# First stage of a transformer block: two weight tiles in halves, low parts of x ahead of the sums of squares, norm's total and spread in the second raw pair

## The reference, cut to what matters

```
def rms_norm(x, g):
    return x * rsqrt(mean(x * x, axis=-1) + EPS) * g
def swiglu(x, w_gate, w_up, w_down):
    return (silu(x @ w_gate) * (x @ w_up)) @ w_down
x = x + 0.5 * swiglu(rms_norm(x, g_ffn1), w_ffn1_gate, w_ffn1_up, w_ffn1_down)
```

## Time and profile before

| what | value |
|---|---|
| median of three runs | 2106.23 us |
| the profiled execution's own time | 2106.04 us |
| its span in the trace | 2103.9 us |
| PE busy | 2088.7 us, 99% of the span |
| DVE busy | 1249.3 us, 59% |
| ACT busy | 793.8 us, 38% |
| POOL busy | 299.6 us, 14% |
| first product of the raw pairs starts | 10.27 us |
| first product of tiles 4 and 5 starts | 35.00 us |

### The profile page before, as it was taken

The page is one execution under the profiler, slowest core; times in us unless marked ns, Lnnn a source line. Parts: engine busy times, 40 slices in busy tenths (PEclk is TensorE's granted clock), DMA queues, the critical chain, the costliest instruction groups (busy, mean ns, idle before and its releaser), DMA issues.

```text
span 2103.9 us, 28233 instructions
## 1 busy us (share of the span) xinstructions
PE 2088.7 (99%) x9928; PEld 1714.0 (81%) x9928; DVE 1249.3 (59%) x1844; ACT 793.8 (38%) x1156; POOL 299.6 (14%) x357
## 2 busy tenths in 40 slices
PE   9999999999999999999999999999999999999999
PEld 8888888887888888877777888888888888888887
DVE  7666544787676654466996676654465466333332
ACT  6222333567432223344365432223343234222222
POOL 0122400650212230024300212210000000000000
PEclk9999999999999999999999999999999999999999
DMA  5565333320345642323300346542323222222232
GB/s 194 180 197 195 93 110 111 118 94 2 110 166 187 198 136 83 96 95 116 102 30 1 110 154 197 190 142 80 97 101 110 91 89 100 100 94 95 76 96 87
DMA packets 79572, 243.32 MB, mean 116 GB/s; under 512 B 12784, under 2 KB 13424, under 8 KB 79376
## 3 DMA queue, kind: packets, MB, share of 16 engines
q1 hardware_dynamic: 61376, 189.61, 27.6%
q0 software_dynamic: 18128, 52.84, 8.1%
HBM read 235.84 MB, written 2.29 MB: 113 GB/s over the span
## 4 chain that ended last, share of the span: by engine, by line
PE 92%; DVE 5%; ACT 1%; POOL 1%; issue 1%; DMA 0%; SPq 0%; ACTq 0%; DVEq 0%; POOLq 0%
PE ps L717 28%; PE ps L719 28%; PE ps L718 28%; PE ps L1027 2%; PE ps L1009 1%; PE ps L988 1%; DVE ps L2012 1%; DVE tmp L1656 1%; DVE small L1910 1%; PE ps L1149 0%; POOL w_lo L626 0%; DVE ropA L1883 0%; PE ps L991 0%; PE ps L933 0%; DVE qA L1885 0%
## 5 line engine op out<-in xcount | busy, mean ns | idle before, releaser
L717 PE MATMUL ps<-h_hi,w_hi 128*128 128x512 f32 x1888 | 740.0, 392 | 1.7 <-DVE h_lo L1955 0.9
L719 PE MATMUL ps<-h_hi,w_lo 128*128 128x512 f32 x1888 | 735.0, 389 | 0.0
L718 PE MATMUL ps<-h_lo,w_hi 128*128 128x512 f32 x1888 | 734.7, 389 | 0.0
L1613 DVE TENSOR_TENSOR w_lo<-w_raw,w_hi 128x1024 fp32r<-128x1024 f32 x336 | 411.4, 1226 | 384.1 <-ACT w_hi L1232 370.1
L1232 ACT ACTIVATE w_hi<-w_raw 128x1024 fp32r<-128x1024 f32 x383 | 402.4, 1052 | 242.5 <-PE ps L719 240.8
L717 PEld LDWEIGHTS ps<-h_hi,w_hi 128*128 128x128 f32 x1888 | 353.7, 187 | 82.4 <-issue 7.7
L719 PEld LDWEIGHTS ps<-h_hi,w_lo 128*128 128x128 f32 x1888 | 353.7, 187 | 75.0
L718 PEld LDWEIGHTS ps<-h_lo,w_hi 128*128 128x128 f32 x1888 | 353.8, 187 | 73.1 <-issue 0.2
L717 PE MATMUL ps<-hid_hi,w_hi 128*128 128x512 f32 x704 | 273.9, 389 | 0.0
L718 PE MATMUL ps<-hid_lo,w_hi 128*128 128x512 f32 x704 | 273.9, 389 | 0.0
L719 PE MATMUL ps<-hid_hi,w_lo 128*128 128x512 f32 x704 | 273.9, 389 | 0.0
(11 more groups left out here) (314 smaller groups left out, 1771.1 us busy)
## 6 DMA issues: line engine op xcount, KB each, us to landing
ada_raw<-in_ada_w POOLq DMA_DIRECT2D x96, 512.0 KB, 4.7
w_raw<-in_gate SPq DMA_DIRECT2D x88, 512.0 KB, 3.5
w_raw<-in_up SPq DMA_DIRECT2D x88, 512.0 KB, 3.2
w_raw<-in_down SPq DMA_DIRECT2D x64, 384.0 KB, 3.1
w_raw<-in_down SPq DMA_DIRECT2D x64, 320.0 KB, 2.9
w_raw<-in_w_mix_c SPq DMA_DIRECT2D x24, 512.0 KB, 3.2
w_raw<-in_w_mix_b SPq DMA_DIRECT2D x17, 512.0 KB, 3.3
w_raw<-in_w_mix SPq DMA_DIRECT2D x16, 512.0 KB, 3.3
```

Of the source, the lines that this page charges most:

```text
L717: pe.matmul(dest, s_hi, m_hi, start=first and n == 0, stop=False)
L718: pe.matmul(dest, s_hi, m_lo, start=False, stop=False)
L719: mm = pe.matmul(dest, s_lo, m_hi, start=False, stop=last and n == len(pairs) - 1)
L1613: dve.tensor_tensor(chunk(w_lo, slot, WT), chunk(w_raw, slot, WT), f32(chunk(w_hi, slot, WT)), ALU.subtract).then_inc(w_lo_done, 1)
```

## The change

The first two weight tiles are loaded, copied and subtracted in halves (chunks 0 to 3, chunks 4 to 7), with semaphores of their own for the first halves, and SP's order becomes: cols, first half of gate 0, x0, first half of up 0, x1, second half of gate 0, x2, second half of up 0, x3, x4, tile 2, x5, x6, x7, tile 3. PE waits for the first halves at chunk 0 and for the second halves at chunk 4. On ACT and DVE the squares and their sums no longer alternate with the high and low parts of x: squares 0 to 3 and sums 0 and 1 stand between the later chunks, and the rest comes after tile 3. The split of tile 3 moves out of `norm` to just before them. PE computes the total after chunk 2 of the second pair (before: chunk 6 of the first) and the spread after chunk 4 of the second pair (before: chunk 0). `idle(30)` becomes `idle(20)`.

```diff
@@ -198,6 +198,9 @@
         x_in = [sem(f"x_in{k}") for k in range(KC)]
         stage_in = sem("stage_in")
         w_in = [sem(f"w_in{s}") for s in range(RING)]
+        w_half_in = [sem(f"w_half_in{s}") for s in range(2)]
+        w_half_hi = sem("w_half_hi")
+        w_half_lo = sem("w_half_lo")
         w_hi_done = sem("w_hi_done")
         w_lo_done = sem("w_lo_done")
         job_done = sem("job_done")
@@ -244,8 +247,8 @@
 
         RAW = {n: first_job[stage] for n, stage in enumerate(("ffn0", "mixA", "ffn1", "mixB", "ffn2", "mixC", "ffn3"))}
         RAW_PAIRS = {n: 2 if n == 0 else 1 for n in RAW}
-        TOTAL_AT = {n: (0, 1) if n else (0, KC - 2) for n in RAW}
-        SPREAD_AT = {n: (0, 2) if n else (1, 0) for n in RAW}
+        TOTAL_AT = {n: (0, 1) if n else (1, 2) for n in RAW}
+        SPREAD_AT = {n: (0, 2) if n else (1, 4) for n in RAW}
         SHIFTED = range(3, 7)
 
         def ada_from(n):
@@ -531,9 +534,16 @@
                         load(J + s, i, 4, tile_of(WEIGHTS[stage], i * 4 + s))
 
             sp.dma_start(cols[:, :], A["cols"]).then_inc(consts_in, 16)
+            def opening_half(s, half, signal):
+                at = half * WT // 2
+                sp.dma_start(w_raw[:, s * WT + at:s * WT + at + WT // 2], A[("gate0", "up0")[s]][0, :, at:at + WT // 2])\
+                    .then_inc(signal, 16)
+
             for k in range(KC):
                 if k < 2:
-                    up_tile(0, 0, k)
+                    opening_half(k, 0, w_half_in[k])
+                elif k < 4:
+                    opening_half(k - 2, 1, w_in[k - 2])
                 sp.dma_start(chunk(x, k), A["x"][k]).then_inc(x_in[k], 16)
                 if k == 4:
                     up_tile(0, 0, 2)
@@ -761,11 +771,17 @@
                     mm.then_inc(p_misc.at(f"shift{n}"), 1)
                 for pair in range(pairs):
                     last = pair == pairs - 1
-                    take(js + 2 * pair + 1)
+                    halved = (n, pair) == (0, 0)
+                    if not halved:
+                        take(js + 2 * pair + 1)
                     for k in range(KC):
                         pe.wait_ge(raw_lo_done, n * KC + k + 1)
+                        if halved and k == KC // 2:
+                            take(js + 1)
                         for s in range(2 * pair, 2 * pair + 2):
                             width = 8 if n == 3 and s == 1 else P
+                            if halved and k == 0:
+                                pe.wait_ge(w_half_lo, s + 1)
                             mm = product(None, bank(s)[0:width, :], [(weights(js + s, k, width),
                                                                        (chunk(hi, k), chunk(lo, k)))], k == 0, k == KC - 1)
                             if k == KC - 1:
@@ -1041,7 +1057,7 @@
                 mm.then_inc(o_turned.at(group), 1)
 
             pe.wait_ge(job_done, RING)
-            idle(30)
+            idle(20)
             pe.wait_ge(prep, 1)
             ffn(0)
 
@@ -1246,9 +1262,7 @@
                     .then_inc(raw_hi_done, 1)
 
             def norm(n, shift):
-                if n == 0:
-                    split(RAW[n] + LEAD, 0, 4)
-                else:
+                if n:
                     act.activation(spare[:, :], flat[:, 0:1], ACT.Sqrt)
                 act.wait_ge(total_done, n + 1)
                 act.activation(token_std[:, :], bank(6)[:, 0:TT], ACT.Sqrt, bias=tiny[:, 0:1], scale=1.0 / D)\
@@ -1449,13 +1463,32 @@
                 act.wait_ge(w_in[w], 16)
                 act.activation(chunk(w_hi, w, WT), chunk(w_raw, w, WT), ACT.Copy).then_inc(w_hi_done, 1)
 
-            first_high(0)
+            def high_half(s, half):
+                at = s * WT + half * WT // 2
+                act.wait_ge(w_in[s] if half else w_half_in[s], 16)
+                act.activation(w_hi[:, at:at + WT // 2], w_raw[:, at:at + WT // 2], ACT.Copy)\
+                    .then_inc(w_hi_done if half else w_half_hi, 1)
+
+            def opening_square(j):
+                if j >= 4:
+                    act.wait_ge(ss_done, j - 2)
+                act.activation(chunk(tmp, j % 4), chunk(x, j), ACT.Square).then_inc(sq_done, 1)
+
+            high_half(0, 0)
             for j in range(KC):
                 act.wait_ge(x_in[j], 16)
                 raw_high(j, col("g_ffn1", 0, KC))
-                if j in (0, 4):
-                    first_high(1 + j // 4)
-                square_x(0, j, j % 2)
+                if j == 0:
+                    high_half(1, 0)
+                if j in (1, 2):
+                    high_half(j - 1, 1)
+                if j == 4:
+                    first_high(2)
+                if j in (3, 4, 5, 6):
+                    opening_square(j - 3)
+            first_high(3)
+            for j in range(4, KC):
+                opening_square(j)
             none = flat[:, 0:KC]
             ffn(0, none, col("g_mix", 0, KC))
 
@@ -1657,8 +1690,6 @@
                             .then_inc(shift_acc.at((n, q, k)), 1)
 
             def norm(n, gain, shift):
-                if n == 0:
-                    split(RAW[n] + LEAD)
                 dve.wait_ge(std_done, n + 1)
                 dve.reciprocal(token_rstd[:, :], token_std[:, :]).then_inc(rstd_done, 1)
                 if n not in (0, 1, 3):
@@ -1981,12 +2012,26 @@
             none, half, whole = (flat[:, n * KC:(n + 1) * KC] for n in range(3))
             clear_sum(0)
             dve.wait_ge(consts_in, 16)
-            split(0)
+            def low_half(s, half):
+                at = s * WT + half * WT // 2
+                dve.wait_ge(w_hi_done if half else w_half_hi, s + 1)
+                dve.tensor_tensor(w_lo[:, at:at + WT // 2], w_raw[:, at:at + WT // 2], f32(w_hi[:, at:at + WT // 2]),
+                                  ALU.subtract).then_inc(w_lo_done if half else w_half_lo, 1)
+
+            low_half(0, 0)
             for j in range(KC):
                 raw_low(0, j, col("g_ffn1", 0, KC))
-                if j in (0, 4):
-                    split(1 + j // 4)
-                sum_x(0, j, j % 2)
+                if j == 0:
+                    low_half(1, 0)
+                if j in (1, 2):
+                    low_half(j - 1, 1)
+                if j == 5:
+                    split(2)
+                if j in (4, 6):
+                    sum_x(0, j // 2 - 2, j // 2 - 2)
+            split(3)
+            for j in range(2, KC):
+                sum_x(0, j, j % 4)
             dve.wait_ge(prep, 1)
             ffn(0, col("g_ffn1", 0, KC), none, half, col("g_mix", 0, KC))
```

## The result

The changed kernel took 2108.4 us (median of 20 runs, 2107.52 to 2113.97) against 2106.2 us (20 runs, 2105.64 to 2110.86) for the kernel before. The ratio is 1.0012, interval 1.0006 to 1.0017: slower by some 2 us, within the 0.2% forecast, 0.6 us above the forecast time. The profiled execution took 2107.58 us.

The account below looks back on a forecast made before the run. PE, busy 99% of the span, was taken as the bound, with its waits. Tiles 4 and 5 later (+0.35) and a clock fall (+1.2) gave +1.55 on the profiled 2106.04, median 2107.8 us; range 2104.6 to 2109.0.

Parts of the forecast that it names:

- The place that decides: In the opening: the time depends on when tiles 4 and 5 can start, forecast 35.35 us instead of 35.00.
- The norm chain moved behind PE's work: Of 11.8 us from total to hidden chunk PE covers 8.6; it stalls 3.2 us ahead of tiles 4 and 5.
- Unit costs: Opening: a product 0.69 us on PE, a chained sum 0.78 on DVE, spread's copy to hidden chunk's end 7.03.
- Tile 2 lands where it did: Opening loads: tile 2 still lands at 11.75 us; two more DMA issues add nothing (bounds 0 and +1.0).
- third rival: Opening loads: tile 2 lands 1.5 us later and the clock falls as well, 2109.8 us; chance 0.10.
- Behind that point all else moves with it: After the first hidden chunk: the rest hangs on the same DVE and PE times and shifts along, adding nothing.
- The clock: PE after the stall: the granted clock more likely than not falls, costing 1.2 us (0 to 1.7).
- The sum: Whole kernel: +0.35 us for the later tiles 4 and 5, +1.2 for the clock, +1.55 together, giving 2107.8 us.
- Full gain: Opening: the norm chain is shorter or hidden and the gain of 3.0 us stays, 2103.2 us; chance 0.12.
- No early start: Opening: PE waits for something else and the first pair starts near 10, about 2108.5 us; chance 0.03.
- Stall without the fall: PE's stall comes but the clock stays at 1.00, 2106.6 us; chance 0.33 of the forecast's 0.75.
- `idle(20)`: PE's start: forty idle records end by 6.3 us, before the first product can start; the removal costs nothing.

Follow-up runs that it names:

- late_norm: The kernel before with only the places of the norm's total and spread moved, after chunks 2 and 4 of the second pair; 2110.04 us against 2105.81, ratio 1.0015.
- splits_first: The changed kernel with tiles 4 and 5 split around the root and reciprocal, the spread one chunk earlier; 2106.64 us against 2106.37 for the kernel before.
- dma_halves: The kernel before with each of the first two weight tiles loaded by two transfers in the old order; 2105.62 us against 2105.81, ratio 0.9997.
- banks_free: The changed kernel with PE's wait ahead of tiles 4 and 5 eased to the scaling out of the banks; 2108.91 us against 2105.81 for the kernel before.
- after_filled13: The changed kernel with 13 idle products on PE ahead of the wait for the first hidden chunk; 2107.82 us against 2107.51 for the kernel before.
- after_again: The changed kernel without an edit, profiled and timed a second time; 2111.62 us against 2107.51 for the kernel before, ratio 1.0016.
- sums_on_pool: The changed kernel with sums of squares on POOL, squares right behind high parts, total and spread earlier; 2114.99 us against 2106.37 for the kernel before.

## Why the prediction was right, point by point

- **The place that decides.** Right. What counts is when tiles 4 and 5 can start. PE's first product came 2.9 us earlier (3.7 forecast; the first chunk of x was there at 5.79, not at 5.0), tiles 4 and 5 came 1.4 us later, and the time followed them.
- **The norm chain moved behind PE's work.** Right, and shown: late_norm makes the stall by the two places alone, and splits_first, with the chain shortened, has 1.67 us of it left. Forecast stall 3.2 us, measured 3.02.
- **Unit costs.** Sums 0.78 forecast, 0.80 measured, so a sum that reads the one before it does cost more than the 0.60 of a sum with another instruction between; total to copy 4.75 forecast, 4.87 measured; copy to hidden chunk 7.03 and 7.04.
- **"Tile 2 lands where it did", "the landing does not feel them".** Wrong by 0.81 us. This term makes up most of the 1.06 us by which tiles 4 and 5 were later than forecast; it was priced in the third rival at +1.5 and held in the range. Ten of the eleven profiles with halves, dma_halves among them, have a later landing than any with whole tiles (12.00 at most); the eleventh has 11.96. That the DMA engines were 0.98 busy said nothing about how much they move, and the two more issues, which the prediction put at nothing, moved tile 2's own issue by 0.91.
- **Behind that point all else moves with it.** Not quite. The second hidden chunk also came late, which added 0.54 us by tile 6. From the end of the first hidden chunk to that of the second DVE takes 11.42 us (36.35 and 47.77), while PE needs 10.88 for tiles 4 and 5: once the first chunk holds PE, the second holds it again. I had worked out only the first wait; banks_free shows that the second was as near.
- **The clock.** Forecast "more likely than not", 1.2 us taken between 0 and 1.7. Measured 1.72 where it fell in late_norm; in the changed kernel it fell in one of two profiles, and there it cost 1.2 more between tiles 4 and 6 (12.64 against 11.42), since it hid the second wait. Three profiles with a filler show no fall and two of the three with the stall do. With one profile of each kernel that speaks for a busy PE preventing the fall but doesn't prove it; the times of after_filled13 and after_again speak for it too.
- **The sum.** +0.35 + 1.2 was forecast. In the first profile, whose clock stayed up, it was +1.41, +0.54 and later -0.45, span +1.5 in all. So it was partly luck that the forecast time came out near the measured one: a missing term (landing and second chunk) stood in for the clock in that execution.
- **Rivals.** Full gain: not seen. No early start: not seen. Stall without the fall: the first profile. Late landing with a fall: after_again (12.77, fall at 37.65), at a smaller size than priced.
- **`idle(20)`** cost nothing visible, but the forecast that its forty records end by 6.3 was wrong: they end at 7.21. They do no harm since the first low part of x is ready only at 7.29 and the first product starts at 7.40. The sum was wrong: by its own rows the 23 records behind the first 17, at 3.41/32 us each, end at 7.2.

The Trainium skill's rule on the matrix engine's clock (TensorE: Matmul & The Clock Gate, HAM oscillation) holds here in part: in two profiles the clock fell to 0.50 behind a wait of 3.0 us. The work did not start at the lower clock, as the page has it; it ran at 1.00 for 0.6 and 1.1 us first. And in a third profile with the same wait there was no fall.

## What to carry to other kernels

An engine that starts earlier needs the chain behind it to move as well: write down, for each wait of the busiest engine in the next stretch, how early its releaser can be, and take the second one too. When a result is needed far from where it is made, the order of the engine that makes it (sums put last, splits written ahead of the copy) can be worth more than the first instruction's time, as it was here. Before cutting a load in pieces, price the pieces on the queue.

## What the runs showed of the hardware

- POOL's additions of 128x512 float32 tiles in SBUF slow DVE's work on such tiles to about half its rate (sums_on_pool): 1.22 us became 2.30, and 0.75 became 1.7. Between two sums on POOL, at 9.49, DVE's subtraction of half a tile took 0.69 again.
- The granted clock also falls late in the program, in some executions of nearly every kernel, with nothing changed there. In late_norm it lasted 10.2 us, in the tail of the second mixer:

```profile
1155.00:1160.00 5.00, 5.00 (x26) 5.00 (x25) 0.00 (x0) 1.19 (x2) 0.00 (x0) 0.50 0.01 3
1160.00:1165.00 5.00, 5.00 (x20) 4.61 (x20) 0.94 (x3) 0.21 (x1) 0.00 (x0) 0.51 0.00 0
```

  The kernel before ran mostly at 2105 to 2107.5 or at 2109 to 2113, with clock means of 0.999 to 1.000 and 0.995 to 0.998; these means point to the same cause, though no profile of it caught such a late fall of 10 us. That is a larger scatter than the change under study, and a median over few runs can take it for an effect.
- A matmul of ones costs 0.11 us in the filler, (38.81 - 35.09)/34. I had sized the filler by 0.08, from 12 records in 1 us of the opening. That was a misreading: a stretch counts every record that overlaps it, at both ends, and the stretches of 1 us from 1 to 10 us of the kernel before hold 81 records while there are 60. So the runs show no difference between the filler and the opening at full clock.
